# One-core transformer kernel: expert choice among 64 sums with bfloat16 lookups, and the engines' split moved to piece 36

## The reference, cut to what matters

```python
s = jnp.einsum('thpd,hpnd->thpn', q, sub_keys).astype(jnp.float32)   # 2 x 128 scores per head
s1, i1 = lax.top_k(s[:, :, 0], 16)
s2, i2 = lax.top_k(s[:, :, 1], 16)
cand_s = (s1[..., :, None] + s2[..., None, :]).reshape(TOK_BLOCK, 8, 256)
cand_i = (i1[..., :, None] * 128 + i2[..., None, :]).reshape(TOK_BLOCK, 8, 256)
top_s, pos = lax.top_k(cand_s, 16)
idx = jnp.take_along_axis(cand_i, pos, axis=-1)
gate = jax.nn.softmax(top_s, axis=-1)
act = jax.nn.gelu(jnp.einsum('thkd,td->thk', expert_u[idx], hb), approximate=False)
out = jnp.einsum('thk,thkd->td', gate * act, expert_v[idx])
```

## Time and profile before

| | |
|---|---|
| median of 3 runs | 1577.87 us (1577.16 to 1578.76) |
| the profiled execution | time 1579.24 us, span 1577.4 us |
| TensorE busy | 1473.9 us, 93% of the span |
| VectorE busy | 1072.0 us, 68% |
| ScalarE busy | 720.6 us, 46% |
| GpSimd busy | 319.8 us, 20% |

### The profile page before, as it was taken

One profiled execution on the slowest core, in us unless ns is written; L12 is line 12 of the kernel. 1 busy time (PEld: TensorE's weight loads), 2 busy tenths in 40 slices (PEclk: granted clock), 3 DMA queues, 4 the chain that ended last, 5 costly groups with the idle time before them and its releaser, 6 DMA issues.

```text
span 1577.4 us, 24907 instructions
## 1 busy us (share of the span) xinstructions
PE 1473.9 (93%) x10282; PEld 1317.8 (84%) x10282; DVE 1072.0 (68%) x1804; ACT 720.6 (46%) x1223; POOL 319.8 (20%) x149
## 2 busy tenths in 40 slices
PE   7997999999998777989999999999999999999998
PEld 6885787998887765877999999999998888888886
DVE  5646554665458878662599988999965555555554
ACT  4555344554353541324454445444444444444443
POOL 0045100000025523056799920000000000000000
PEclk9998999999999988969999999999999999999999
DMA  7623342455553410024465554444455656666663
GB/s 275 209 92 103 115 160 91 161 185 192 187 157 116 120 53 2 1 67 133 151 203 170 174 161 148 148 148 147 146 163 161 188 188 188 188 189 189 188 188 122
DMA packets 64880, 235.25 MB, mean 149 GB/s; under 512 B 7424, under 2 KB 7680, under 8 KB 64512
## 3 DMA queue, kind: packets, MB, share of 16 engines
q1 hardware_dynamic: 63904, 231.60, 46.1%
q10 hardware_dynamic: 864, 2.07, 0.4%
HBM read 232.60 MB, written 1.05 MB: 148 GB/s over the span
## 4 chain that ended last, share of the span: by engine, by line
PE 80%; DVE 11%; POOL 4%; ACT 3%; issue 2%; DMA 1%; ACTq 0%; DVEq 0%; POOLq 0%
PE ps L129 78%; POOL spl L144 3%; ACT spl L141 1%; PE ps L138 1%; DVE junk L144 1%; DVE spl L144 1%; DVE prep L144 1%; DVE pm L144 1%; DMA raw<-in_w_in_a 1%; DVE pR L144 1%; DVE pm L153 1%; DVE hx L144 1%; DMA par<-in_par 1%; DVE be L144 0%; DVE ez L144 0%
## 5 line engine op out<-in xcount | busy, mean ns | idle before, releaser
L129 PE MATMUL ps<-xhl,spl 128*128 128x256 f32 x4944 | 609.6, 283 | 11.3 <-POOL spl L144 9.6
L129 PEld LDWEIGHTS ps<-xhl,spl 128*128 128x128 f32 x4944 | 593.9, 189 | 15.1 <-POOL spl L144 11.3
L141 ACT ACTIVATE spl<-raw 128x1024 fp32r<-128x1024 f32 (+1 forms) x435 | 454.2, 1048 | 328.9 <-PE ps L129 311.2
L144 DVE TENSOR_TENSOR spl<-raw,spl 128x1024 fp32r<-128x1024 f32 (+1 forms) x329 | 402.3, 1229 | 214.5 <-ACT spl L141 212.7
L129 PE MATMUL ps<-spl,Wr 128*128 128x512 f32 x1536 | 360.1, 396 | 3.3 <-DVE Wr L144 3.3
L129 PEld LDWEIGHTS ps<-spl,Wr 128*128 128x128 f32 x1536 | 289.3, 188 | 73.9 <-DVE Wr L144 3.6
L144 POOL TENSOR_TENSOR spl<-raw,spl 128x1024 fp32r<-128x1024 f32 (+1 forms) x106 | 274.9, 2609 | 297.6 <-ACT spl L141 297.1
L141 ACT ACTIVATE Wr<-GE 128x256 fp32r<-128x256 f32 x128 | 53.5, 419 | 184.9 <-PE ps L129 184.9
L141 ACT ACTIVATE GE<-ps 128x256 f32<-128x256 f32 (+42 forms) x176 | 57.1, 327 | 126.5 <-DVE GE L144 109.9
L144 DVE TENSOR_TENSOR Wr<-GE,Wr 128x256 fp32r<-128x256 f32 x128 | 54.4, 426 | 82.8 <-ACT Wr L141 82.8
L129 PE MATMUL ps<-spl,ahl 128*128 128x512 f32 x384 | 90.1, 396 | 0.0
(11 more groups left out here) (337 smaller groups left out, 1245.9 us busy)
## 6 DMA issues: line engine op xcount, KB each, us to landing
raw<-in_eu SPq DMA_DIRECT2D x128, 512.0 KB, 3.6
raw<-in_ev SPq DMA_DIRECT2D x128, 512.0 KB, 3.7
raw<-in_w_up SPq DMA_DIRECT2D x32, 512.0 KB, 3.6
raw<-in_w_down SPq DMA_DIRECT2D x32, 512.0 KB, 4.2
raw<-in_w_in_a SPq DMA_DIRECT2D x16, 512.0 KB, 5.6
raw<-in_w_pq SPq DMA_DIRECT2D x16, 512.0 KB, 3.5
raw<-in_w_rwkv SPq DMA_DIRECT2D x14, 512.0 KB, 3.8
raw<-in_w_in_t SPq DMA_DIRECT2D x8, 512.0 KB, 3.5
```

Source lines behind the costliest of these rows:

```text
L129: return Done(self, self.e and self.e.matmul(out, l, r, start=st, stop=sp))
L141: return Done(self, self.e and self.e.activation(out, a, f, bias=bias, scale=scale, accum_out=acc))
L144: return Done(self, self.e and self.e.tensor_tensor(out, a, b, op))
```

## The change

There are three edits, all in the expert part.

1. *The sums.* Only 64 of the 256 sums are made: rank 0 of s1 with 16 of s2, ranks 1 to 3 with 8, ranks 4 to 7 with 4, ranks 8 to 15 with 1, in four adds. `top16(8, ...)` searches rows of 64.
2. *The lookups.* The places (0 to 127), the positions (0 to 63) and the ranks are held in bfloat16, which has them exactly. Thirteen short instructions turn a position into its two ranks (minima and maxima over the four ranges). A lookup is a compare and a multiply laid out so that all tensors have step 1, and four adds that halve the candidates (8, 4, 2, 1) in place of the reduce. Tables are cast twice over into pairs (`xb`). `io16` is a new bfloat16 constant, cast once.
3. *The split of work.* `EU_POOL` goes from 44 to 36: VectorE makes the low parts of the pieces of `eu` from 36. `CHOICE` goes from 42 to 36, `GATES` from 47 to 41.

```diff
--- before.py
+++ after.py
@@ -22,8 +22,8 @@
          ("w_lora", 1, 1024, 0), ("w_rwkv_1", 6, 1024, 1), ("w_mla", 8, 672, 1), ("w_uq", 3, 768, 1), ("w_ukv", 2, 1024, 1), ("w_o", 8, 1024, 1),
          ("w_pq", 16, 1024, 1), ("sub_keys", 2, 1024, 0), ("eu", 128, 1024, 1), ("ev", 128, 1024, 1)]
 ON_POOL = ("w_pq", "w_o", "w_xk", "w_xv", "w_rwkv_0", "w_rwkv_1", "w_mla")
-EU_POOL = 44
-CHOICE, GATES, NGRP = 42, 47, 64
+EU_POOL = 36
+CHOICE, GATES, NGRP = 36, 41, 64
 PIECES = [(nm, j, n, sp) for nm, cnt, n, sp in ORDER for j in range(cnt)]
 AT = {nm: i for i, (nm, j, _, _) in enumerate(PIECES) if j == 0}
 SPLIT = [i for i, p in enumerate(PIECES) if p[3]]
@@ -449,15 +449,19 @@
         sS2 = ST_("sS2", [128, 16, 128])
         m16 = ST_("m16", [128, 16, 16])
         ix = ST_("ix", [128, 16, 16], U32)
-        ixf = ST_("ixf", [128, 16, 16])
+        xb = ST_("xb", [128, 2, 8, 16, 2], BF16)
+        io16 = ST_("io16", [128, 16, 16], BF16)
         top = ST_("top", [128, 8, 16])
         pst = ST_("pst", [128, 8, 16], U32)
         psi = ST_("psi", [128, 2, 128], U32)
-        psf = ST_("psf", [128, 2, 128])
+        pos_ = ST_("pos_", [128, 3, 128], BF16)
+        pij = ST_("pij", [128, 2, 128], BF16)
+        pt = ST_("pt", [128, 3, 128], BF16)
         sel = ST_("sel", [128, 2, 3, 128])
         gs = ST_("gs", [128, 2, 2, 8])
-        cand = qP[:, 0:8, :].rearrange("p h (a b) -> p h a b", b=16)
-        cand2 = qP[:, 8:16, :]
+        Sq = Mem(nc, ge_at + 65536, ge_at + 65536 + 16384)
+        cand, cand2 = Sq("cand", [128, 8, 64]), Sq("cand2", [128, 8, 64])
+        eq, eqx = (Sq(f"eq{j}", [128, 8, 16, 16], BF16) for j in range(2))
         x32 = sS2[:, :, :].rearrange("p a b -> p (a b)").rearrange("p (k t) -> p k t", k=8)
         s_x5 = [stat(2) for _ in range(2)]
         o_fin = GE[:, 0:8, :].rearrange("p a b -> p (a b)").rearrange("p (t n) -> p t n", t=2)
@@ -2398,22 +2402,45 @@
                 dve.wait_ge("xs_l")
                 dve.wait_ge("w_used", AT["sub_keys"] + 1)
                 top16(16, lambda i: sS[:, tb, i, :], lambda i: sS2[:, i, :], m16, ix)
-                v1 = dve.cp(ixf[:, :, :], ix[:, :, :]).own()
+                x4 = ix[:, :, :].rearrange("p (h c) k -> p c h k", c=2)
+                for j in range(2):
+                    v1 = dve.cp(xb[:, j, :, :, :], bc(x4[:, j, :, :], 3, 2)).own()
                 mv = m16[:, :, :].rearrange("p (h c) k -> p h c k", c=2)
-                xv = ixf[:, :, :].rearrange("p (h c) k -> p h c k", c=2)
-                dve.after(dve.tt(cand, bc(mv[:, :, 0, :], 3, 16), bc(mv[:, :, 1, :], 2, 16), ALU.add).own())
-                top16(8, lambda i: cand[:, i, :, :].rearrange("p a b -> p (a b)"), lambda i: cand2[:, i, :], top, pst)
+                for at, i0, i1, n in ((0, 0, 1, 16), (16, 1, 4, 8), (40, 4, 8, 4), (56, 8, 16, 1)):
+                    o = cand[:, :, at:at + (i1 - i0) * n].rearrange("p h (a b) -> p h a b", b=n)
+                    v = dve.tt(o, bc(mv[:, :, 0, i0:i1], 3, n), bc(mv[:, :, 1, 0:n], 2, i1 - i0), ALU.add).own()
+                dve.after(v)
+                top16(8, lambda i: cand[:, i, :], lambda i: cand2[:, i, :], top, pst)
                 sg_ = sel[:, tb, 2, :].rearrange("p (h k) -> p h k", k=16)
                 dve.tt(sg_, top[:, :, :], bc(top[:, :, 0], 2, 16), ALU.subtract).then_inc("sel_sub", tb)
                 pf = pst[:, :, :].rearrange("p h k -> p (h k)")
-                dve.ts1(psi[:, 0, :], pf, 4, ALU.logical_shift_right)
-                dve.after(dve.ts1(psi[:, 1, :], pf, 15, ALU.bitwise_and).own())
-                dve.after(dve.cp(psf[:, :, :], psi[:, :, :]).own())
-                eqf = cand.rearrange("p h a b -> p (h a) b")
+                dve.cp(pos_[:, 2, :], pf)
+                dve.ts1(psi[:, 0, :], pf, 3, ALU.logical_shift_right)
+                dve.after(dve.ts1(psi[:, 1, :], pf, 2, ALU.logical_shift_right).own())
+                dve.after(dve.cp(pos_[:, 0:2, :], psi[:, :, :]).own())
+                dve.after(dve.ts(pt[:, 0, :], pos_[:, 0, :], -1.0, 0.0, ALU.add, ALU.max).own())
+                dve.after(dve.stt(pt[:, 1, :], pos_[:, 1, :], -6.0, pt[:, 0, :], ALU.add, ALU.max).own())
+                i_ = pij[:, 0, :]
+                dve.after(dve.stt(i_, pos_[:, 2, :], -48.0, pt[:, 1, :], ALU.add, ALU.max).own())
+                dve.ts(pt[:, 2, :], i_, 4.0, 24.0, ALU.mult, ALU.add)
+                dve.after(dve.ts(pt[:, 0, :], i_, 8.0, 8.0, ALU.mult, ALU.add).own())
+                dve.after(dve.stt(pt[:, 1, :], i_, 16.0, pt[:, 0, :], ALU.mult, ALU.min).own())
+                dve.after(dve.tt(pt[:, 0, :], pt[:, 2, :], pt[:, 1, :], ALU.min).own())
+                dve.after(dve.stt(pt[:, 1, :], i_, 48.0, pt[:, 0, :], ALU.add, ALU.min).own())
+                dve.after(dve.tt(pij[:, 1, :], pos_[:, 2, :], pt[:, 1, :], ALU.subtract).own(), v1)
                 for j in range(2):
-                    dve.after(dve.tt(eqf, bc(psf[:, j, :], 2, 16), bc(C("iota16"), 1, 128), ALU.is_equal).own(), v1)
-                    dve.after(dve.tt(cand, cand, bc(xv[:, :, j, :], 2, 16), ALU.mult).own())
-                    dve.after(dve.red(sel[:, tb, j, :], eqf, ALU.add).then_inc("sel", tb))
+                    dve.after(dve.tt(eq[:, :, :, :], bc(pij[:, j, :].rearrange("p (h k) -> p h k", k=16), 2, 16), bc(io16[:, :, :], 1, 8), ALU.is_equal).own())
+                    v = dve.tt(eqx[:, :, :, :].rearrange("p h a (b c) -> p (h a) b c", c=2), eq[:, :, :, :].rearrange("p h a (b c) -> p (h a) b c", c=2),
+                               bc(xb[:, j, :, :, :].rearrange("p h a c -> p (h a) c"), 2, 8), ALU.mult).own()
+                    for n in (8, 4, 2):
+                        dve.after(v)
+                        v = dve.tt(eqx[:, :, 0:n, :], eqx[:, :, 0:n, :], eqx[:, :, n:2 * n, :], ALU.add).own()
+                    dve.after(v)
+                    o = sel[:, tb, j, :].rearrange("p (h k) -> p h k", k=16)
+                    dve.after(dve.tt(o, eqx[:, :, 0, :], eqx[:, :, 1, :], ALU.add).then_inc("sel", tb))
                 yield
                 dve.wait_ge("sel_exp", tb)
                 dve.after(dve.red(gs[:, tb, 0, :], sg_, ALU.add).own())
@@ -2468,6 +2495,8 @@
 
             dve.wait_ge("h4")
             dve.cp(io2[:, :, :], bc(C("iota"), 2, 2)).own()
+            dve.wait_ge("x32")
+            dve.cp(io16[:, :, :], bc(C("iota16"), 2, 16)).own()
             ch = [choose(0), choose(1)]
             for x in ch:
                 next(x)
```

## The result

The changed kernel takes 1590.62 us in the median of 4 runs (1588.30 to 1592.72), the kernel before 1578.32 (1577.16 to 1579.09). The ratio is 1.0078, with a 95% interval of 1.0060 to 1.0097: slower by 12.3 us, inside the forecast's range and on its side. The profiled execution is the fastest of the four (1588.30 us, span 1586.5), 9.1 us of time and of span above the profiled one of before.

The account below looks back on a forecast made before the run. TensorE was taken to bound the kernel, busy 1473.9 of 1577.4 us. Old stops gone -6.4, new stop at piece 36 +22.2 and clock +1.7 gave +17.5 us, so 1595 us; the forecast's own range was 1588 to 1604.

Parts of the forecast that it names:

- (d): VectorE's position to rank pair: 14 short dependent instructions with the subtraction, 3.5 us per half alone, taking turns with GpSimd.
- (e): VectorE's table lookups: 12 bfloat16 instructions per half, 8.6 us alone, 34 us in half one beside GpSimd's splits.
- how many pass in a pause: Short VectorE instructions getting through between GpSimd's splits: bounds one to three, taken as 2.5 per 2.84 us, 22.7 us.
- the old stops: Six TensorE stops for GpSimd's low half, at `eu` pieces 18 to 21 and 39 to 42: 6.4 us together.
- (g): GpSimd's lateness inside half one: shorter holds no longer make it stop TensorE, so six stops vanish, -6.4 us.
- The clock: TensorE's lower granted clock behind the long stop at piece 36: +1.7 us, at least 0, at most double.
- Gates from piece 41: The 64 gates groups starting at piece 41: same count, same 1 us stop ahead of them, no cost.
- (1): Rival, chance 0.16: the choice is done by 886.3, TensorE never stops at piece 36, 1571.5 us.
- (2): Rival, chance 0.12: two-input bfloat16 instructions take no turn with GpSimd; stop of 4 to 7 us, 1575 to 1580.
- (3): Rival, chance 0.04: one VectorE instruction per GpSimd split throughout; stop 40 us at piece 36, 1613 us.
- My sign against myself: In VectorE's lookups: compares of 1.2 us beside GpSimd splits of 2.40 would show the forecast wrong.

Follow-up runs that it names:

- run 3: Changed kernel with GpSimd's low halves of the `eu` pieces cut to 8 of 1024 columns: 1570.39 us, ratio 0.9956 to the kernel before.
- run 4: Changed kernel with one reduce in place of each lookup's four halving adds: 1584.14 us, ratio 1.0042 to the kernel before.
- run 5: Changed kernel with eight extra instructions ahead of half one's lookups: bfloat16 minima 1595.05 us, or f32 reduces 1588.61 us.
- run 1: Changed kernel with the old places (`EU_POOL` 44, `CHOICE` 42, `GATES` 47), so the new choice alone: 1576.89 us, ratio 1.000 to the kernel before.
- run 2: Kernel before, old choice kept, with only the new places (`EU_POOL` 36, `CHOICE` 36, `GATES` 41): 1587.47 us, ratio 1.0060 to the kernel before.
- run 6: Changed kernel with one reduce per lookup and the old places (44, 42, 47): 1571.37 us, ratio 0.9953 to the kernel before.
- run 7: Changed kernel with both tables' lookups done by the same instructions and the old places (44, 42, 47): 1575.16 us, ratio 0.9977 to the kernel before.

## Why the prediction was right

**The mechanism and the place.** The forecast was one stop of some 20 us for VectorE's split at piece 36 and none for GpSimd ahead of it; the profile has one of 16.1 to 16.4 and none. The step on which it hung, (d) and (e), that instructions which share with GpSimd are to be counted and not timed, is shown by runs 3, 4 and 5: 35 us of half one vanish with GpSimd's splits, and eight more cost 8.5 or 2.6 us by their kind.

**Mis-sized: how many pass in a pause.** I took 2.5 per 2.84 us for the 20 short ones, 22.7 us. They took 16.9: two to four passed from one split to the next, three on average (14 in 12.8 us), which is the upper bound that I read from the earlier trace rows. Of the four adds of the sums, which do not depend on one another, one passed ahead of a split and three behind it, 3.1 us in all. Of the 8.0 us by which half one was forecast too long (82.5 for 74.5), 5.8 come from this term and 2.3 from the lookups (34 for 31.7). Half two was 2 us longer than forecast, since half one ended 8 us sooner and the adds of half two still met GpSimd's last split (3.10 us for four; 0.89 in run 3, where nothing holds them). So the stop was sized 22.2 for 16.35.

**Mis-sized: the old stops.** In (g) I added the idle times in the brackets, 6.4 us. By starts they cost 8.1: a matmul's end is modelled, so the bracket leaves out what the starts show. Both errors made the forecast too high: 17.5 against 9.8 in the profiles, 1595 against 1590.62. That the times lie nearer to each other (17.5 forecast, 12.3 between the medians) is luck: the 2.5 us by which the medians differ more than the rows add up to are explained by no row.

**The clock** was sized right, 1.7 for 1.6 us, once; a mean of 0.55 over the first 4 us is the lower level for most of them. In part that is luck: counted in the same way, the stops of runs 1, 2, 4 and 5 (by starts 5.0, 11.8, 12.7, 22.8 and 16.9 us) cost 2.4, 1.8, 2.4, 1.8 and 1.3 us, in no order of their length. The stops of up to 1.3 us cost none (granted clock 1.00 behind them in the kernel before and in runs 6 and 7). **Gates from piece 41** cost nothing that shows: the stop ahead of the first gates is 0.98 us in both, and the sum of the other terms is what the `ev` matmuls start later.

**The rivals.** That it fits (1) failed by 16.4 us: it needed the choice done 100.9 us behind the first `eu` matmul (886.3 - 785.4), and it took 117.3. That bfloat16 with two inputs takes no turn (2) is refuted by the eight minima. One per split throughout (3) holds inside the lookups, not for the short ones. My sign against myself, a compare of 1.2 us beside a split, did appear once, at 828.55; it speaks for the turns all the same, since the split was the one that waited (3.48 us).

The Trainium skill, SBUF — State Buffer, section Who interferes with whom, states that a VectorE instruction with two SBUF inputs contends with a GpSimd instruction that reads SBUF, that whoever issues first holds the shared ports for the whole instruction, and that `tensor_reduce` on trn2 never contends. The runs agree for bfloat16 too (eight minima of 0.22 us took 8.46) and for f32 reduces (eight of 0.29 us took 2.54); the bfloat16 reduce of run 4 took 4.41 us beside GpSimd and 3.81 alone, which the rule does not explain.

## What to carry to other kernels

Beside an engine with which yours takes turns by whole instructions, count the instructions that must take a turn. Where the other engine has its next instruction queued, price each at one of that engine's: here an add of 0.29 us cost 2.4. Where it pauses in between, some slip through: here three per pause, so 0.9 to 1.1 us each. A faster form built of many small instructions can be the slower one, and a single slow reduce that takes no turn the better one. When work moves to an engine that is in the middle of a long run, compare the end of that run with the first date on which the moved work is due.

## What was not expected of the hardware

A reduce over bfloat16 with a step of 16 elements took 3.81 us for 2048 elements, 2.29 for the f32 one with step 1. Beside GpSimd it took up to 4.41, while GpSimd's split that began next to it ran in 2.44: something holds such a reduce for up to 0.6 us, and no run here tells what. Nor does one tell whether the type or the step makes the 3.81.
